# Softmax row sums in a three-layer transformer kernel: 64-fold reciprocals turned by TensorE in place of sixteen small products per pair of heads

## The reference

```python
logits = jnp.einsum('bhqd,bhkd->bhqk', qc, k).astype(jnp.float32)
...
p = jax.nn.softmax(logits, axis=-1).astype(v.dtype)
return jnp.einsum('bhqk,bhkd->bhqd', p, v)
```

```python
denom = jnp.sum(p, axis=-1, keepdims=True) + jnp.exp(sink - m)
```

## Time and profile before

| | |
|---|---|
| Median of 3 runs | 2175.9 us (2173.77 to 2177.2) |
| The profiled execution, its own time | 2173.69 us |
| Its span in the trace | 2171.9 us |
| TensorE matmul busy | 2106.6 us (97%) |
| VectorE busy | 1268.6 us (58%) |
| ScalarE busy | 938.9 us (43%) |
| Granted TensorE clock, mean over the span | 0.995 of full |

### The profile page before, as it was taken

One profiled execution on the slowest core, in us unless ns is written; L12 is line 12 of the kernel. 1 busy time (PEld: TensorE's weight loads), 2 busy tenths in 40 slices (PEclk: granted clock), 3 DMA queues, 4 the chain that ended last, 5 costly groups with the idle time before them and its releaser, 6 DMA issues. The chain is left out here.

```text
span 2171.9 us, 30675 instructions
## 1 busy us (share of the span) xinstructions
PE 2106.6 (97%) x11441; PEld 1749.7 (81%) x11441; DVE 1268.6 (58%) x2133; ACT 938.9 (43%) x1898; POOL 33.9 (2%) x71
## 2 busy tenths in 40 slices
PE   7999999999999898999999999999999889999999
PEld 7899777888889676788888888888888667888887
DVE  7655567737755775776477544344448856443542
ACT  7655444424445764543244343223344654322331
POOL 0000001000001000000000000000001000000000
PEclk9999999999999999999999999999999999999999
DMA  6221123332233011233322323323332112333332
GB/s 214 79 59 54 50 78 97 107 97 88 97 98 97 16 35 35 74 102 103 91 97 97 102 93 98 101 92 98 97 96 65 30 45 88 97 99 96 97 97 93
DMA packets 101669, 187.36 MB, mean 86 GB/s; under 512 B 11408, under 2 KB 12048, under 8 KB 101264
## 3 DMA queue, kind: packets, MB, share of 16 engines
q1 hardware_dynamic: 101520, 185.39, 27.6%
HBM read 183.25 MB, written 2.10 MB: 85 GB/s over the span
## 5 line engine op out<-in xcount | busy, mean ns | idle before, releaser
L1795 DVE TENSOR_TENSOR WL<-RAW,WH 128x512 fp32r<-128x512 f32 x681 | 458.7, 690 | 357.9 <-ACT WH L2069 336.5
L1625 PE MATMUL PSA<-HNh,WH 128*128 128x512 f32 x1440 | 563.8, 392 | 5.6 <-DVE HNl L1784 4.2
L1627 PE MATMUL PSA<-HNh,WL 128*128 128x512 f32 x1440 | 560.3, 389 | 0.0
L1626 PE MATMUL PSA<-HNl,WH 128*128 128x512 f32 x1440 | 560.3, 389 | 0.0
L2069 ACT ACTIVATE WH<-RAW 128x512 fp32r<-128x512 f32 x681 | 413.1, 625 | 312.7 <-PE PSA L1627 221.3
L1625 PEld LDWEIGHTS PSA<-HNh,WH 128*128 128x128 f32 x1440 | 270.3, 188 | 66.7 <-DVE HNl L1784 7.6
L1627 PEld LDWEIGHTS PSA<-HNh,WL 128*128 128x128 f32 x1440 | 270.3, 188 | 56.8
L1626 PEld LDWEIGHTS PSA<-HNl,WH 128*128 128x128 f32 x1440 | 270.3, 188 | 56.6 <-issue 1.2
L1625 PE MATMUL PSA<-Gh,WH 128*128 128x512 f32 x704 | 274.1, 389 | 2.1 <-DVE Gl L1964 2.1
L1626 PE MATMUL PSA<-Gl,WH 128*128 128x512 f32 x704 | 273.9, 389 | 0.0
L1627 PE MATMUL PSA<-Gh,WL 128*128 128x512 f32 x704 | 273.9, 389 | 0.0
(11 more groups left out here) (255 smaller groups left out, 2439.0 us busy)
## 6 DMA issues: line engine op xcount, KB each, us to landing
RAW<-in_w SPq DMA_DIRECT2D x681, 256.0 KB, 2.6
XT<-in_x SPq DMA_DIRECT2D x8, 256.0 KB, 5.2
MT<-in_mem SPq DMA_DIRECT2D x2, 1024.0 KB, 6.9
out_x<-XT SPq DMA_DIRECT2D x8, 256.0 KB, 2.0
PAR<-in_par SPq DMA_DIRECT2D x1, 207.0 KB, 7.2
CB<-in_cb SPq DMA_DIRECT2D x1, 100.0 KB, 7.2
PAR<-in_par SPq DMA_DIRECT2D x1, 84.5 KB, 2.0
CONST<-in_const SPq DMA_DIRECT2D x1, 65.0 KB, 5.7
```

What stands on the lines that cost most here:

```text
L1625: pe.matmul(out, wh, xh, start=(a["start"] and c == 0), stop=False)
L1626: pe.matmul(out, wh, xl, start=False, stop=False)
L1627: p = pe.matmul(out, wl, xh, start=False, stop=ends)
L1795: dve.tensor_tensor(l[:, :], r[:, :], h[:, :], ALU.subtract).then_inc(done.sem("split.dve"), 1)
```

## The change

The reciprocals are no longer kept as 8 columns. `precip` writes each 64 times over: one VectorE instruction reads the 8 row sums through a broadcast pattern (4 blocks x 2 heads x 64) and writes 128 x 512 reciprocals to a buffer of `TMP` (slot `inv`). `pbcast` is then four transposes of 128 x 128 of that buffer. `PSTAT` becomes free after `precip`, not after `pbcast`; `TMP` serves two takers per pair, and `precip` waits until its buffer is free.

```diff
@@ score
                 if u == 0:
-                    pstats.take(jkey, [("pbcast.pe", jkey)])
+                    pstats.take(jkey, [("precip.dve", jkey)])
@@ sums
-                step("pbcast", jkey, S=PSTAT[pstats.of[jkey]], bank=aux)
+                step("pbcast", jkey, inv=TMP[tmp.of["inv", jkey]], bank=aux)
@@ recip
-                step("precip", jkey, job=job, S=S, last=self.end(n))
+                i = tmp.take(("inv", jkey), [("pbcast.pe", jkey)])
+                step("precip", jkey, job=job, S=S, inv=TMP[i], before=tmp.before["inv", jkey], last=self.end(n))
@@ tensor: pbcast
                     for i in range(4):
-                        for x in range(2):
-                            p = pe.matmul(PS[a["bank"]][64 * x:64 * x + 64, 128 * i:128 * i + 128],
-                                          a["S"][:, x, 3, i:i + 1].broadcast_to([128, 64]), IDENT, start=True, stop=True)
+                        c = slice(128 * i, 128 * i + 128)
+                        p = pe.transpose(PS[a["bank"]][:, c], a["inv"][:, c], IDENT)
@@ vector: precip
-                    dve.reciprocal(St[:, :, 3, :], St[:, :, 1, :]).then_inc(done.sem("precip.dve"), 1)
+                    for t in a["before"]:
+                        w.wait_ge(*done(*t))
+                    dve.reciprocal(a["inv"][:, :].rearrange("p (i x d) -> p i x d", i=4, x=2),
+                                   St[:, :, 1, :].rearrange("p x i -> p i x").unsqueeze(3).broadcast_to(
+                                       [128, 4, 2, 64])).then_inc(done.sem("precip.dve"), 1)
```

## The result

The changed kernel takes 2215.2 us (median of 4 runs, 2213.79 to 2216.24), against 2174.8 us for the kernel before (4 runs): 1.018 times as long, interval 1.0172 to 1.0196, or 40 us more. The profiled execution took 2216.02 us with a span of 2214.2 us.

A forecast was written before the change was run, and what follows sets the result against it. TensorE was taken to bound the kernel. Its saving of 2 us, 28 us of waits for a 3.0 us reciprocal and 5 us of lower clock gave +31 on 2175.9, about 2207 us; range for 8 in 10: 2174 to 2225.

The forecast's parts named there:

- What bounds the kernel: Whole kernel: TensorE, with a matmul in 97% of the span; VectorE has little room in mla and block 2.
- Removed and added on TensorE: `pbcast`: four transposes at 0.85 us replace sixteen product records at 0.92 us or more, 2.1 us off in all.
- faster: Rival on `pbcast`: transposes at 58 ns a record save 0.46 us a pair, 10 us in all, giving 2166; chance 0.04.
- parallel half-width tiles: Old products on TensorE: tiles of a divided array work in parallel, which would explain 58 against 106 ns a record.
- Added on VectorE: `precip`: the 128x512 reciprocal costs per element and takes 3.0 us (2.3 to 3.7), 62 us more of VectorE.
- fixed-cost rival: `precip`: the reciprocal's extra 36 ns are fixed, so it takes 0.73 us; 2175.5 us, no change; chance 0.17.
- estimate of 4.4 us: `precip`: eight steps of 1.04 ns an element; as a rival, 52 us of waits and 2233 us; chance 0.08.
- Who waits for it: TensorE in fox, mla and block 2: 19.5 us of direct delay plus 15 from the queue behind the reciprocal, together 35.
- the prediction's two counts: Waits of TensorE: 19.5 us directly for the reciprocals, and 15 us added by the queue behind them on VectorE.
- I let a fifth go: Of the 35 us of waits, a fifth is swallowed by waits TensorE already has, which leaves 28 us.
- The clock: After waits of over 2 us TensorE runs partly at 1.2 GHz: three or four stretches, up to 1.4 us each, 5 us.
- The sum: Whole kernel: -2 saved on TensorE, +28 of waits, +5 for the clock, +31 us, about 2207 us.

The follow-up runs named there:

- e2: Kernel before, its sixteen-record products kept but waiting for an added, unread 128x512 VectorE reciprocal (the 8-column one is made too): 2225.1 us, ratio 1.0237.
- e10: Changed kernel with the reciprocal on 8 columns and a GpSimd copy spreading it to 128x512 for the four transposes: 2171.4 us, ratio 0.998.
- e3: Kernel before plus an unread 128x512 reciprocal on VectorE behind the 8-column one; the products wait only for the 8-column one: 2225.0 us, ratio 1.0231.
- e11: Changed kernel with an 8-column reciprocal and the GpSimd spreading copy done four times before it signals, so the operand comes late: 2194.5 us, ratio 1.0088.
- e9: Changed kernel with an 8-column reciprocal and the GpSimd spreading copy done five times before it signals, so the operand comes late: 2219.4 us, ratio 1.0198.
- e8: Changed kernel with 159 unread bf16 products on TensorE ahead of the transposes of 14 pairs, to fill its waits: 2221.2 us, ratio 1.0212.

## Why the prediction was right or wrong

The direction was right and the time lies within the range: 2215 us against 2207 forecast, in 2174 to 2225. Taken by its own steps:

**What bounds the kernel: right.** The stages that had idle time lost 33 us between their first and last reciprocals, and fox with its near full TensorE 5 to 6. But time in which TensorE doesn't wait is not all alike: some of it ran slower, which is taken up under the clock.

**Removed and added on TensorE: wrong, and mis-sized by a factor of five.** "Four full transposes of the same kind ... 0.85 us" were eight, since the step took an fp32 transpose for two records. The saving is about 10 us (e2 less the changed kernel, and 9.7 by the rows of e10), not 2.1, about 0.4 us a pair. The number stood in the prediction as the rival "faster" (0.46 us a pair, 10 us), set aside for the wrong reading of the same rows. Its support for parallel half-width tiles is void too: one half-width product took 115 ns (two records) and one full transpose 106. The Trainium skill says in "TensorE: Matmul & The Clock Gate", in its table of terms, that transposes of fp32 have a mode of their own that is 4 times faster. The runs here agree in direction, with one record against two; a factor of 4 is not shown.

**Added on VectorE: right in kind, its size a tenth small.** A reciprocal costs per element: 202 ns for 8 elements, 1701 for 256, 3352 for 512. From the first to the last that is (3352 - 202) / 504 = 6.25 ns an element, against 5.54 forecast from 8 elements, and the range of 2.3 to 3.7 us held. The fixed-cost rival (0.73 us) fell. The estimate of 4.4 us by the repeat count of 8 in "VectorE: DVE Perf Modes" of the Trainium skill, first walkthrough, was too long: measured is 3.35.

**Who waits for it: right in size, partly by luck in its parts.** For the direct wait the prediction had 19.5 us at a delay of 3.05; the trace has 19.8 in 12 places. That agreement is partly luck: transposes that have to wait start 3.4 us after the reciprocal does, and at a delay of 3.4 the prediction's own leads give 25 us. The rows behind the reciprocal do arrive, as it said for `YK` (3.2 us) and the exponentials (14.4 us where there were 12.0). The copies of `PT` directly behind it arrive too, which the prediction doesn't name: TensorE waits 9.4 us for them at lines 1713 and 1757, where the kernel before had 2.0 at line 1712 and none at its `pbcast`. In all TensorE's time without a matmul grew by 32 us, against 28 forecast. At 3.35 us the prediction's two counts, taken between its 35 us at 3.0 and 49 at 3.7, give 42 us, and 34 with the fifth taken off.

Adding to the direct wait of a pair only what the queue has beyond it, as the prediction did, agrees with that sum. What can't be done is to read the two parts as what would go if one were taken away. e3 took the direct wait away and kept the queue, and the loss stayed at 51 us. e11 kept the direct wait and took the queue away: 23 us. The two are in large part the same delay seen in two places: held VectorE alone carries the whole loss, and the direct wait lies inside it.

**"I let a fifth go": about right in the sum.** In e11 TensorE waits 22.7 us for the copies, and its time without a matmul is 19.1 us above that of e10; in e9 it is 37.3 and 31.2. About a sixth is swallowed in both.

**The clock: right in sign, its term some three times too small.** In mla and block 2 the granted clock fell from 0.98 and 0.96 to 0.92 and 0.87, under the prediction's bound of 0.97. Its price can be read where TensorE has the same instructions to work off. Its busy time grew by 20.7 us from the kernel before to e3, by 14.5 to e2, by 13.3 from e10 to the changed kernel, by 15.4 to e9, and by 2.8 to e11, whose clock is that of e10. In e3 11.6 of the 20.7 us lie in mla, where 1021 records took 131.8 us at 0.98 before and 143.4 at 0.91. So of the 50 us that the wide reciprocal costs, 14 to 21 are work done slower and 31 to 36 time without a matmul. The prediction charged 5 us for the first, three or four stretches. That all of the slower work is the clock's is read from its place and from the products of e3 that took 1.77 us for 0.92; no run held the clock up while TensorE waited, since e8 left it where it was. Why the clock fell lower in e3 than in e2 is open.

**The sum.** Forecast -2 + 28 + 5 = +31; measured -10 saved, +36 without a matmul and +14 slower (e2) = +40. The saving was 8 us too small, the waits 8 and the clock 9. The first has the opposite sign of the other two, so the total was closer than its terms, which is luck.

## What to carry to other kernels

Work put on an engine that is in the loop of waits costs its length minus the lead of whatever stands behind it, and the leads are used up once: half the duration cost a third here, and the second half cost all of its length. Take the leads of the whole queue behind the instruction, not only of its reader, and take for each place the longer delay of the two, not their sum. Price the work that follows the waits as well: here a fourth to two fifths of the loss was TensorE's own work at the lower clock, which no list of waits shows; comparing the engine's busy time on the same instructions does. A reciprocal is paid by the element: take it of the few values and spread the result by a copy, on an engine with room; and count instructions from the program before reading a time per record from a trace.

## What the runs showed of the hardware

- A VectorE reciprocal of fp32 takes 202 ns for 128x8, 1701 for 128x256, 3352 for 128x512: about 6.25 ns an element (6.04 up to 256, 6.45 beyond). At 128x512 that is 4.9 times an ordinary operation of that form (690 ns).
- Copying 8 columns 64-fold to 128x512 fp32, SBUF to SBUF, takes 427 ns on VectorE, against 690 for an operation on two tensors (the weight split); 628 on average on ScalarE and 647 on GpSimd. "VectorE: DVE Perf Modes" of the Trainium skill, in its tier table of the perf modes, says that a copy of fp32 within SBUF runs at twice the rate; 427 against 690 agrees, if part of both is fixed, also where the source is broadcast.
- An fp32 transpose of 128x128 is one record, an fp32 product two. Eight transposes in a row take 106 ns each; the four of a pair 0.58 us with what surrounds them.
- TensorE's busy time rose while its work fell (2106.6 to 2117.1 us with 264 records less), since it counts time at either clock. It can't be used for work done where the clock moves.
- The same sixteen records of products took 0.92 us in the kernel before and 1.77 in e3, behind a wait of 3.29 us, at a granted clock of 0.50.
